# The second memory projection spread over the attention steps of the first layer, in a fused transformer kernel

## The reference

```python
mem_n = rmsnorm(mem, norm_mem)
for i in range(DEPTH):                      # DEPTH = 2
    h = rmsnorm(x, norm_mix[i])
    mkv = mem_n @ w_mem_kv[i]               # 256 x 1024 @ 1024 x 512: keys and values of the memory
    mk, mv = mkv[..., :mw], mkv[..., mw:]
    ...
    y_tok = windowed_gqa(q, k, v, sink_a[li])      # i = 0: softmax with a window, ALiBi and a sink
    y_mem = memory_attn(qm, mk, mv)                # 4 heads over 256 memory tokens
    x = x + concat([y_tok, y_mem]) @ w_out[i]
    ...                                             # gated FFN
```

## Time and profile before

| | |
|---|---|
| median of 3 runs | 1112.36 us (1109.6 to 1112.61) |
| the profiled execution | 1111.92 us |
| its span | 1110.1 us |
| PE busy | 1041.9 us (94% of the span) |
| DVE busy | 738.4 us (67%) |
| ACT busy | 587.1 us (53%) |
| POOL busy | 116.8 us (11%) |
| mean granted clock of PE | 0.975 |
| share of the chain that ended last | PE 73%, DVE 9%, ACT 7%, issue 4%, DMA 4% |

### The profile page before, as it was taken

How to read it: one execution, slowest core, us unless ns; L and a number is a source line. 1 busy time by engine, 2 the same in 40 slices (tenths; PEclk the granted TensorE clock), 3 DMA queues, 4 the chain that set the end, 5 groups by cost and what they waited for, 6 DMA issues and landing times.

```text
span 1110.1 us, 13563 instructions
## 1 busy us (share of the span) xinstructions
PE 1041.9 (94%) x5224; PEld 864.3 (78%) x5224; DVE 738.4 (67%) x984; ACT 587.1 (53%) x834; POOL 116.8 (11%) x159
## 2 busy tenths in 40 slices
PE   5997996999999999899999999998989989999996
PEld 5876875888888777788888888787767778888885
DVE  4667773465455567578888656669867766777753
ACT  6547562444345557544443445467656456666631
POOL 1013130000000013110000011012551000000001
PEclk9998998999999999999999979999999989999999
DMA  9655378655556441379999784435463535465441
GB/s 335 227 141 71 113 206 211 203 195 182 176 172 208 152 153 39 114 258 366 335 337 328 296 264 151 159 121 172 160 199 114 190 133 190 154 193 184 157 147 38
DMA packets 97825, 209.28 MB, mean 189 GB/s; under 512 B 5650, under 2 KB 13282, under 8 KB 94626
## 3 DMA queue, kind: packets, MB, share of 16 engines
q1 hardware_dynamic: 93313, 194.46, 52.0%
q0 software_dynamic: 4288, 13.89, 5.6%
q10 hardware_dynamic: 160, 0.07, 0.0%
HBM read 205.25 MB, written 4.57 MB: 189 GB/s over the span
## 4 chain that ended last, share of the span: by engine, by line
PE 73%; DVE 9%; ACT 7%; issue 4%; DMA 4%; POOL 2%; SPq 1%; ACTq 0%; DVEq 0%; POOLq 0%
PE bank L855 21%; PE bank L857 21%; PE bank L856 21%; PE bank L833 4%; ACT hi L1175 3%; DVE lo L1600 3%; DMA big<-scratch_rpb 2%; PE bank L869 2%; PE bank L835 1%; POOL big L1885 1%; PE bank L969 1%; DMA raw<-in_w_down 1%; DVE xres L1475 1%; DMA small<-in_sink_a 1%; DMA scratch_rpb<-in_rpb_b 1%
## 5 line engine op out<-in xcount | busy, mean ns | idle before, releaser
L1600 DVE TENSOR_TENSOR lo<-raw,hi 128x2048 fp32r<-128x2048 f32 (+1 forms) x164 | 367.4, 2242 | 219.1 <-ACT hi L1175 218.4
L1175 ACT ACTIVATE hi<-raw 128x2048 fp32r<-128x2048 f32 (+1 forms) x164 | 303.5, 1852 | 203.7 <-PE bank L857 156.9
L855 PE MATMUL bank<-hi,xTh 128*128 128x512 f32 (+2 forms) x896 | 346.9, 387 | 10.4 <-DVE lo L1600 10.4
L857 PE MATMUL bank<-hi,xTl 128*128 128x512 f32 (+2 forms) x896 | 337.7, 377 | 0.0
L856 PE MATMUL bank<-lo,xTh 128*128 128x512 f32 (+2 forms) x896 | 337.6, 377 | 0.0
L855 PEld LDWEIGHTS bank<-hi,xTh 128*128 128x128 f32 x896 | 170.3, 190 | 42.2 <-DVE lo L1600 11.0
L857 PEld LDWEIGHTS bank<-hi,xTl 128*128 128x128 f32 x896 | 170.0, 190 | 31.7
L856 PEld LDWEIGHTS bank<-lo,xTh 128*128 128x128 f32 x896 | 170.6, 190 | 28.6 <-issue 0.2
L855 PE MATMUL bank<-hi,hTh 128*128 128x512 f32 x264 | 103.5, 392 | 0.5 <-DVE lo L1600 0.5
L857 PE MATMUL bank<-hi,hTl 128*128 128x512 f32 x264 | 102.8, 389 | 0.0
L856 PE MATMUL bank<-lo,hTh 128*128 128x512 f32 x264 | 102.8, 389 | 0.0
(11 more groups left out here) (348 smaller groups left out, 1358.5 us busy)
## 6 DMA issues: line engine op xcount, KB each, us to landing
raw<-in_w_gate_up SPq DMA_DIRECT2D x44, 1024.0 KB, 5.4
raw<-in_w_down SPq DMA_DIRECT2D x30, 1024.0 KB, 5.1
raw<-in_w_ada SPq DMA_DIRECT2D x24, 1024.0 KB, 6.4
raw<-in_w_up SPq DMA_DIRECT2D x22, 1024.0 KB, 5.1
raw<-in_w_in SPq DMA_DIRECT2D x21, 1024.0 KB, 5.1
raw<-in_w_out SPq DMA_DIRECT2D x12, 1024.0 KB, 5.0
raw<-in_w_in_b SPq DMA_DIRECT2D x10, 1024.0 KB, 5.1
raw<-in_w_in_a SPq DMA_DIRECT2D x6, 1024.0 KB, 10.0
```

The source lines that it names most:

```text
L855: e.matmul(o, sh, h[:, k, :], start=p.first and k == 0, stop=False)
L857: done = e.matmul(o, sl, h[:, k, :], start=False, stop=p.last and k == p.nk - 1)
L1175: e.activation(hi_s[m % SPLITS][:, 0:n], raw[p.at % RAWS][:, 0:n], ACT.Copy).then_inc(hi_made, 1)
L1600: e.tensor_tensor(lo_s[s][:, 0:n], raw[p.at % RAWS][:, 0:n], hi_s[s][:, 0:n].bitcast(F), ALU.subtract).then_inc(lo_made, 1)
```

## The change

`linear` takes a list for `pops`: the n-th call of `between` then takes as many entries from the queue as the n-th number says. The second memory projection gets `[4, 2, 4]` where it had 1.

```diff
@@ linear
-        hooks = deque(hooks or [])
+        hooks, each = deque(hooks or []), deque(pops if isinstance(pops, list) else [])
         def between():
-            if hooks:
+            if each:
+                self.pop(each.popleft())
+            elif hooks:
@@ mix, l == 0
             self.put("rel")
-            self.linear("mem", 1, 0, 512, 2, "mem", 1)
+            self.linear("mem", 1, 0, 512, 2, "mem", [4, 2, 4])
```

## The result

| | before | after the change |
|---|---|---|
| median | 1110.72 us (1108.01 to 1116.08, 20 runs) | 1115.35 us (1111.54 to 1119.69, 20 runs) |
| ratio of the times | | 1.0038, 95% interval 1.0026 to 1.0051 |
| the profiled execution, its span | 1111.92, 1110.1 us | 1113.81, 1112.0 us |
| mean granted clock of PE | 0.975 | 0.971 |

The change makes the kernel slower by 0.38%, some 4 us. The same kernel, timed once more beside the second group of experiments, gave 1.0046 (1.0030 to 1.0061), some 5 us.

What follows compares the result with a forecast made beforehand. The attention stage was taken as bound by a DVE-ACT chain, one round a step. Terms: -6.45 start, +3.94 split, +3.6 last quarter and evacuation, +3.0 clock: 4.1 us slower, 1116.0 us, range 1111.5 to 1119.5 us.

Steps and rivals of the forecast that it cites:

- The earlier start: Step 4 of attention opens on DVE at 74.8 instead of 81.25 us, a gain of 6.45 us.
- The wait ahead of step 4's scores: PE newly waits some 2.8 us for DVE's lows of keys, which does not hurt the chain by itself.
- The split inside the chain: Part 13's copies on ACT and DVE now stand ahead of step 7 and cost 3.94 us.
- no cover: ACT's idle time hides none of the split's 3.94 us, since DVE's half waits for ACT's.
- The low half of part 13 at 84 us: Sign in the profile after: DVE makes this half at about 84 us, between two steps.
- The last quarter and the evacuation: Queued behind step 8's scores, the quarter ends at 96.2 us; its evacuation delays step 9 to 98.0 us, costing 3.6 us.
- the walk without the clock: Start, split, last quarter and evacuation together, without clock falls: step 9 opens later, taken as 1.1 us.
- two short falls: PE drops to its lower clock behind two waits, at step 4's and step 8's scores: 3.0 us; chance 0.45.
- two long falls: Rival: both clock falls last long, 3.1 us each, giving 7.3 us slower, 1119.2 us; chance 0.13.
- the overlap works: Rival: DVE and ACT absorb split and evacuation, 1105.5 us, or 1109.4 us with the split paid; chance 0.07.
- The clock stays up, or falls once: Rival: PE's work is spread evenly, leaving 1.1 us, or 2.6 with one short fall: 1113.0 to 1114.5 us; chance 0.35.

Runs made afterwards that it cites:

- the short copy: The change with both copies of part 13 cut to 256 of 2048 columns: 1113.07 us, 1.0022; the same cut in the kernel before: 1110.12 us, 1.0000.
- the clock kept up: The change plus unread extra matmuls in PE's waits: 1114.36 us (1.0034), then 1112.98 us (1.0020); the same kind in the kernel before: 1110.60 us (0.9995).
- the list [3, 4, 2]: The change with [3, 4, 2] for [4, 2, 4], so quarter 3 follows step 7 and quarter 4 precedes step 8: 1110.19 us (0.9987), then 1109.13 us (0.9976).

## Why the prediction was right

It gave 1116.0 us on the profiled 1111.92, 4.1 us slower; measured are 0.38% and 0.46%, 4.2 and 5.1 us. The mechanism is the one it named. That the first number is met to 0.1 us is luck: the interval of the ratio alone goes from 2.9 to 5.7 us, and the two traces of the change have a delay of the stage of 5.46 and 2.56 us. Its steps one by one:

- **The earlier start, 74.8 us:** 74.59. Right.
- **The wait ahead of step 4's scores, 2.8 us:** 3.44, released by the lows of the keys as said.
- **The split inside the chain, 3.94 us:** 3.35 us for seven eighths of it at step 7. Right there, and free in the kernel before. But the prediction took "no cover", and in the trace of the short copy only 2.1 of the 3.35 us reach the lows of queries, since PE is still at quarter 3.
- **The low half of part 13 at 84 us:** 86.37 in the change, 84.08 with the clock kept up. With part 12 set level, 2.5 us lie between them, and they are the first fall of the clock: quarter 2 took 4.75 us, ACT waited 3.43 us for the products behind it, and DVE for ACT. The chain of causes is the prediction's. Its 1.5 us for a short fall were too little in the first trace and right in the second (86.48 us, 1.5 us late once part 12 is set level).
- **The last quarter and the evacuation:** with the clock kept up DVE waits 3.00 us ahead of the evacuation, as the prediction had it ("some 3 us"), and step 9 opens at 98.90, 98.85 with part 12 set level, instead of the 98.0 counted. 1.0 us of it is what the extra matmuls cost. So the walk without the clock is 1.1 us by the prediction and 1.1 us by the runs (97.85 - 96.79). That the scores of step 8 now wait for all four lows of queries is seen too: they start 1.81 us behind the first of them (92.34, 94.15 us in the second trace), against 1.08 before.
- **The clock, two short falls for 3.0 us:** this is the weakest term, though the sum hardly shows it. By the traces it is 4.4 us in one execution (5.46 - 1.06, the delay with the clock kept up and the extra matmuls taken off) and 1.5 us in the other; by the ratios it is 2.7 us, with an interval from 1.0 to 4.4. As a mean the 3.0 us may well be right, but the falls differ from execution to execution, and neither trace shows two short ones: the first has two long falls, which cost 4.4 us and not the 6.2 counted for that rival, the second has one fall ahead of step 9. And the second fall did not hit the last quarter, which ran at full speed, but the turns, the scores and the products by the values ahead of it.
- **The start of the span.** Against 5.46 us of delay the span grew by 1.9 us only in the profiled pair. 2.2 us went at the bias table's transfer. Most of the rest went from 651 to 671 us, where the trace of before has a longer fall of the clock: the granted clock from 640 to 720 us is 0.89 before and 0.94 after. The medians do not rest on one execution.

Of the rivals, "the overlap works" is out: the evacuation waits in every run in which the last quarter stands behind step 8. In the list [3, 4, 2] it works in part, for 2.2 us, which says that the rule of interleaving was not wrong here, but its place. The Trainium skill, Perfetto Trace Analysis, section "Optimization Strategy", says that a kernel with several regimes may gain by interleaving them; the two runs of that list agree (0.9987, whose interval still reaches 1, and 0.9976), and the change at 1.0038 shows where it fails, when what is put in waits behind the chain's own products.

"The clock stays up, or falls once" is nearer than its time says. The second traced execution is its case, with one fall on the path and a delay of 2.56 us, which it put at 2.6. But the medians, 1115.35 and 1117.45 us, lie above its 1113.0 to 1114.5 us. Such times were measured when extra matmuls kept the clock up (1114.36 and 1112.98).

What stays open: how the 4.7 us of the change's ratios part between clock and order to better than 1.7 us, and why the short copy gave 0.5 us in its trace and 2.7 in its ratio.

## What to carry to other kernels

When work is moved into a chain that goes back and forth between two engines, ask for each moved piece what it stands behind on its own engine: a quarter queued behind scores that wait for DVE can't be ready when DVE comes to it, however much idle time PE has. Put copies and evacuations where the chain has a break anyway, several at once. And when an experiment needs scratch memory, take it from a buffer that exists, or run the buffer alone beside it.

## What the runs showed of the hardware

**A buffer of 8 bytes a row cost 0.62% (0.40 to 0.84), 7 us.** It stands ahead of the buffers `hTh`, `qyh` and others in memory, and no instruction differs otherwise. PE at 330 us in the kernel before, where `hTh` and `hTl` are multiplied (0.227 us from start to start, 2.27 us over ten):

```profile
329.71 0.39 PE L856 MATMUL bank<-lo,hTh 128*128 128x512 f32 x1
...
331.98 0.39 PE L857 MATMUL bank<-hi,hTl 128*128 128x512 f32 x1
```

and with the buffer (0.234 us, 2.34 us over ten), at the same granted clock:

```profile
329.69 0.40 PE L857 MATMUL bank<-lo,hTh 128*128 128x512 f32 x1
...
332.03 0.40 PE L858 MATMUL bank<-hi,hTl 128*128 128x512 f32 x1
```

The groups of the same stretch, 310 to 460 us, say which matmuls it is: those of `hTh`, whose buffer comes behind the new one, take 399 ns instead of 393, those of `xTh`, whose buffer comes ahead of it, 402 and 403. First before, then with the buffer (count, busy us, mean ns):

```profile
L855 PE MATMUL bank<-hi,xTh 128*128 128x512 f32 x80 | 32.2, 403 | 0.0
...
L855 PE MATMUL bank<-hi,hTh 128*128 128x512 f32 x49 | 19.3, 393 | 0.0
```

```profile
L856 PE MATMUL bank<-hi,xTh 128*128 128x512 f32 x80 | 32.2, 402 | 0.0
...
L856 PE MATMUL bank<-hi,hTh 128*128 128x512 f32 x50 | 19.9, 399 | 0.0
```

The operand that moved is the block of 128 x 128 from the activations; `hi` and `lo` lie ahead of the new buffer in both kernels. So a matmul's pace depends on where that operand lies in memory. Which places are slow wasn't tried.

**The same transfer differs by up to 2.7 us between executions.** The bias table's took 17.65 us in the kernel before, 15.86 and 17.31 in the two traces of the change, and from 15.51 to 18.17 us over all fourteen traces. A difference of a us or two behind it, between two single traces, says nothing about what stands ahead of it.

**A fall of the clock is not a fixed thing of the kernel.** The same program had PEclk 0.51 from 91 to 98 us in one execution and 1.00 from 91 to 103 in the other, behind a wait of the same length (1.88 us in both) and around a second one of 1.14 and 1.57 us. The Trainium skill, TensorE: Matmul & The Clock Gate, section "What's actually happening", says that activity releases the throttle; the runs with PE kept busy agree, with 1.00 from 66 to 107.6 us in all three traces.
